# A rotation table for the S5 layer: built in place between the experts of the first expert stage, instead of during the input projection with a trip through DRAM

## What is computed

```python
mag = jnp.exp(dt * a_r)
ab_re = mag * jnp.cos(dt * a_i)
ab_im = mag * jnp.sin(dt * a_i)
...
_, _, hr, hi = lax.associative_scan(combine, (a_re_b, a_im_b, bu_re, bu_im), axis=1)
```

## Time and profile before

| what | us |
|---|---|
| median of 3 runs | 1224.56 (1222.78 to 1225.12) |
| the profiled execution, its own time | 1224.22 |
| its span, first to last instruction | 1222.4 |
| busy in it: PE, DVE, POOL, ACT | 932.2, 449.6, 300.4, 186.0 |
| mean granted TensorE clock | 0.817 of full speed |

### The profile page before, as it was taken

One profiled execution on the slowest core, in us unless ns is written; L12 is line 12 of the kernel. 1 busy time (PEld: TensorE's weight loads), 2 busy tenths in 40 slices (PEclk: granted clock), 3 DMA queues, 4 the chain that ended last, 5 costly groups with the idle time before them and its releaser, 6 DMA issues.

```text
span 1222.4 us, 11170 instructions
## 1 busy us (share of the span) xinstructions
PE 932.2 (76%) x4366; PEld 546.2 (45%) x4366; DVE 449.6 (37%) x757; ACT 186.0 (15%) x313; POOL 300.4 (25%) x439
## 2 busy tenths in 40 slices
PE   7999947988886488888778528999743987787870
PEld 5888737775642233333323427964211333233330
DVE  4899974535124411111011247620254111111116
ACT  1311300121111111111001323210111110011111
POOL 3799915502002321111110210000031111111110
PEclk9999966897578689898889755559955998888895
DMA  9457273020403779999999742430172899999953
GB/s 234 143 202 252 108 237 138 1 78 10 139 14 142 305 272 388 407 412 414 410 409 418 306 121 70 138 103 10 67 289 92 348 409 407 406 410 406 421 223 140
DMA packets 77797, 290.28 MB, mean 237 GB/s; under 512 B 25913, under 2 KB 44807, under 8 KB 62486
## 3 DMA queue, kind: packets, MB, share of 16 engines
q1 hardware_dynamic: 63530, 260.45, 55.4%
q10 hardware_dynamic: 9092, 20.42, 4.9%
q0 software_dynamic: 5120, 8.66, 2.1%
HBM read 267.92 MB, written 28.50 MB: 242 GB/s over the span
## 4 chain that ended last, share of the span: by engine, by line
PE 63%; DVE 20%; issue 8%; DMA 5%; ACT 2%; SPq 1%; POOLq 0%; POOL 0%; ACTq 0%; DVEq 0%
PE ps L1592 20%; PE ps L1611 9%; PE ps L2145 5%; PE ps L1574 3%; DVE work L478 3%; PE ps L838 2%; PE ps L316 2%; PE ps L2008 2%; PE ps L2023 2%; DMA ring<-s_out_mats 2%; DVE work L1121 1%; DVE ring L1124 1%; PE ps L551 1%; PE ps L817 1%; PE ps L565 1%
## 5 line engine op out<-in xcount | busy, mean ns | idle before, releaser
L1592 PE MATMUL ps<-ring,work 128*64 128x512 f32 x512 | 256.6, 660 | 76.8 <-issue 75.4
L1593 PE MATMUL ps<-ring,work 128*64 128x512 f32 x512 | 257.1, 660 | 0.0
L1592 PEld LDWEIGHTS ps<-ring,work 128*64 128x64 f32 x512 | 74.8, 152 | 223.1 <-issue 220.8
L1632 DVE TENSOR_TENSOR work<-ps,work 64x512 f32<-64x512 f32 x32 | 34.1, 1066 | 348.0 <-ACT work L1621 348.0
L1611 PE MATMUL ps<-ring,work 128*64 128x512 f32 x256 | 116.6, 598 | 1.4 <-DVE work L1637 1.4
L1612 PE MATMUL ps<-ring,work 128*64 128x512 f32 x256 | 116.6, 598 | 0.0
L316 PE MATMUL ps<-work,ring 128*128 128x264 f32 x512 | 115.2, 387 | 0.0
L316 PEld LDWEIGHTS ps<-work,ring 128*128 128x128 f32 x512 | 96.8, 190 | 16.4
L1128 POOL TENSOR_TENSOR ring<-ring 128x512 f32<-128x512 f32 (+6 forms) x88 | 96.8, 1118 | 5.7 <-DVE ring L1107 2.1
L1654 POOL COPY work<-work 64x1 int32<-64x1 int32 x32 | 5.7, 178 | 289.6 <-PE ps L1574 243.5
L1593 PEld LDWEIGHTS ps<-ring,work 128*64 128x64 f32 x512 | 74.7, 152 | 0.0
(11 more groups left out here) (456 smaller groups left out, 1367.8 us busy)
## 6 DMA issues: line engine op xcount, KB each, us to landing
ring<-in_moe_w_gate SPq DMA_DIRECT2D x32, 2048.0 KB
ring<-in_moe_w_up SPq DMA_DIRECT2D x32, 2048.0 KB
ring<-in_moe_w_down SPq DMA_DIRECT2D x32, 2048.0 KB, 24.3
ring<-in_w_in ACTq DMA_DIRECT2D x6, 2048.0 KB, 9.0
s_out_mats<-ring SPq DMA_DIRECT2D x4, 1280.0 KB, 4.9
ring<-s_out_mats SPq DMA_DIRECT2D x1, 5120.0 KB, 22.9
ring<-in_w_in SPq DMA_DIRECT2D x2, 2048.0 KB, 10.3
s_in_mats<-ring SPq DMA_DIRECT2D x4, 1024.0 KB, 6.0
```

What stands on the lines that cost most here:

```text
L1592: nc.tensor.matmul(ps[0:SLOT, 2 + s, :], xgT[s][:, c], gate_w[s][:, c], start=c == 0, stop=c == DC - 1)
L1593: last = nc.tensor.matmul(ps[SLOT:P, 2 + s, :], xgT[s][:, c], up_w[s][:, c], start=c == 0, stop=c == DC - 1)
L1632: nc.vector.tensor_tensor(hid[s][0:SLOT].rearrange("t (c p) -> t p c", c=4), strided(ps[SLOT:P, 2 + s, :]), strided(sg[s][SLOT:P]), ALU.mu ...
```

## The change

The table is no longer made during the projection, stored and loaded. `s5_turn_dve`, its store, the wait for the store and `s5_turn_load` are gone. POOL's two squarings move from `s5_prep_pool` to the end of `s5_early_pool`, with three products in place of four (ten instructions on 32 to 64 elements per partition, in four dependent groups). DVE fills `E5` in place during the first expert stage: the start after expert 1's copy of the hidden rows, then one part of one doubling (three instructions) after that of each of the experts 2 to 13. POOL's first copies out of the B matrices after that stage (`s5_mat_pool`) wait for the table, since its scratch lies there. In `ring`, the scratch tiles of the preparation lie elsewhere.

```diff
@@ ab_dve_project
                                   ps[0:11, 5:8, :]).then_inc(*dv.done("conv_rest"))
-            s5_turn_dve(v)
@@ s5_prep_pool
-            nc.gpsimd.tensor_copy(turn[:, 0], pcols[:, 0:2]).then_inc(*po.done())
...
-            cmul(one(1), one(0), one(0), 1)
-            cmul(one(2), one(1), one(1), 1, "turn4")
             cmul(W8[:, :, 2:4], W8[:, :, 0:2], W8[:, :, 1:2], 2)
@@ s5_prep_stores
-            q.wait_ge(*dv.at("turns"))
-            q.dma_start(E_dram, E_ab.rearrange("p w t n -> p (w t n)")).then_inc(sem("E_out"), 16)
             q.wait_ge(sem("cols_out"), 16)
-            q.wait_ge(sem("E_out"), 16)
@@ moe_dve
                 dve_hidT(v, l, *at_expert(k))
+                if l == 0 and k == 1:
+                    s5_turn_start(v)
+                if l == 0 and 2 <= k < 14:
+                    s5_turn_step(v, (k - 2) // 2, k % 2)
@@ s5_turn_load and the functions in its place
-        def s5_turn_load(q):
-            q.wait_ge(sem("stores_S"), 16)
-            q.dma_start(E5.rearrange("p w t n -> p (w t n)"), E_dram).then_inc(sem("E_in"), 16)
+        def s5_turn_start(v):
+
+            v.wait_ge(*po.at("turn4"))
+            v.wait_ge(sem("stores_S"), 16)
+            nc.vector.tensor_copy(E5[:, :, :, 0].rearrange("p w (r k) -> p w r k", r=4),
+                                  turn[:, 1].rearrange("p w (k r) -> p w r k", r=4)).then_inc(*dv.done())
+
+        def s5_turn_step(v, b, w):
+
+            n = 2 ** b
+            tmp = [view(work, F["Bb"] + 1024 * i, PT, 32) for i in range(2)]
+            re, im = (E5[:, i, :, 0:n] for i in range(2))
+            cr, ci = (E5[:, i, :, n - 1:n].to_broadcast([P, PT, n]) for i in range(2))
+            (x, y), (z, o), op = (((re, cr), (im, ci), ALU.subtract), ((re, ci), (im, cr), ALU.add))[w]
+            v.wait_ge(*dv.last())
+            nc.vector.tensor_tensor(tmp[0][:, :, 0:n], x, y, ALU.mult).then_inc(*dv.done())
+            nc.vector.tensor_tensor(tmp[1][:, :, 0:n], z, o, ALU.mult).then_inc(*dv.done())
+            v.wait_ge(*dv.last())
+            nc.vector.tensor_tensor(E5[:, w, :, n:2 * n], tmp[0][:, :, 0:n], tmp[1][:, :, 0:n], op).then_inc(*dv.done("turns"))
@@ s5_early_pool
             tt(abh[:, 1], T8[:, 2], T8[:, 3], ALU.add, "abh")
+            pool.wait_ge(*po.last())
+            x, t = pcol[:, 0:2], T8[:, 0]
+            for i in range(2):
+                for j, (a, b) in enumerate(((0, 0), (1, 1), (0, 1))):
+                    tt(t[:, j], x[:, a], x[:, b], ALU.mult)
+                pool.wait_ge(*po.last())
+                tt(turn[:, i, 0], t[:, 0], t[:, 1], ALU.subtract)
+                tt(turn[:, i, 1], t[:, 2], t[:, 2], ALU.add, "turn4")
+                pool.wait_ge(*po.last())
+                x = turn[:, i]
@@ s5_mat_pool
             pool.wait_ge(sem("Bm_in"), 16)
+            pool.wait_ge(*dv.at("turns"))
@@ s5_dve
-            v.wait_ge(sem("E_in"), 16)
             v.wait_ge(*po.at("abh"))
@@ the SP list
             sp.wait_ge(*pe.at("mixAB2"))
-            s5_turn_load(sp)
             moe_weights(sp, "n0", 0)
```

More of the change, by code:

```diff
@@ L959, in ab_stores @@
                 sp.dma_start(out["s_C"][:, 0, h].rearrange("b k v -> k b v"), Cst[:, h * NS:(h + 1) * NS]).then_inc(sem("stores_C"), 16)
-        S5P = carve(ring, 0, rows=2560, cols=256, ldt=8, W8=512, ZW=256, P5=480, turn=192, Bn=1024, CT=1024,
-                    E=4096, stB=2048, stC=2560)
+        S5P = carve(ring, 0, rows=2560, cols=256, ldt=8, W8=512, ZW=256, P5=480, Bn=1024, CT=1024,
+                    Cn=2048, stB=2048, stC=2560)
         assert S5P["end"] <= 16384, S5P["end"]
@@ L975, in build @@
         P5 = view(ring, S5P["P5"], 3, 5, PT)
-        turn = view(ring, S5P["turn"], 3, 2, PT)
         Bn = view(ring, S5P["Bn"], 2, PT, C5)
-        Cn = view(ring, S5P["E"], 2, DC, 2, N5)
+        Cn = view(ring, S5P["Cn"], 2, DC, 2, N5)
         CT = view(ring, S5P["CT"], 2, PT, C5)
-        E_ab = view(ring, S5P["E"], 2, PT, N5)
         stB = view(ring, S5P["stB"], 2, DC, 4, 2, C5)
         stC = view(ring, S5P["stC"], 2, DC, 5, 2, C5)
-        E_dram = dram("turns", (P, 2 * PT * N5))
         B_dram = dram("s5_in_mats", (4, P, 2048))
@@ L1107, in s5_ct_dve @@
                     nc.vector.tensor_copy(CT[at, :, 8 * n:8 * n + 8], src).then_inc(*dv.done(f"CT{n}"))
[L1109 to L1124, removed]
         def s5_prep_pool(pool):
@@ L1148, in s5_prep_pool @@
             pool.wait_ge(*po.last())
-            one = lambda i: turn[:, i].unsqueeze(2)
-            cmul(one(1), one(0), one(0), 1)
-            cmul(one(2), one(1), one(1), 1, "turn4")
             cmul(W8[:, :, 2:4], W8[:, :, 0:2], W8[:, :, 1:2], 2)
@@ L1808, in build @@
         K1 = carve(work, A["raw"], abh=2 * PT * NS, pcol=8 * PT, h0s=2 * NS * PT, dI=DC * 32, hs=2 * PT * NS, hl=2 * PT,
-                   hout=6 * P, mag=2 * PT, id4=3 * 32)
+                   hout=6 * P, mag=2 * PT, id4=3 * 32, turn=4 * PT)
         assert K1["end"] <= A["cv"], K1["end"]
@@ L1819, in build @@
         id4 = view(work, K1["id4"], 3, 32)
+        turn = view(work, K1["turn"], 2, 2, PT)
         F = carve(work, M["end"], Bb=2048, E=4096, m4=2048)
```

## The result

Before and after, in four runs each: 1224.84 us (1222.78 to 1225.94) and **1206.99 us** (1206.20 to 1207.59). The ratio is 0.9856, interval 0.9839 to 0.9873: the change takes 17.9 us off, more than the 14.5 of the forecast and inside its range. The profiled execution after took 1207.26 us, with a span of 1205.5.

The account below looks back on a forecast made before the run. State loads waiting for DVE's table and its store were taken to bound the stretch before line 551. 14.9 us earlier there, less 0.4 for the routing, made 14.5: 1209.7 profiled, median 1210.0, range 1203.5 to 1216.5.

Parts of the forecast that it names:

- The landing in place of the table's wait: Between the last batch's store and the first state load: the store lands in 4.9 us (4.4 to 5.5).
- POOL's batches: POOL's work before the last store: 3.5 us earlier, 3.0 from batches beside a silent DVE, 0.5 from fewer products.
- The far end: Upper bound for the gain in POOL's batches: 6 us, at 2 ns per element, as line 730 with DVE idle.
- Load to line 551: From the first state load's issue to PE's start of line 551: kept at 18.0 us.
- The floor: PE ends lines 523 to 543 at 165.9, 4.6 us before the states; the gain cannot pass 19.5 us.
- The routing: POOL's ten moved instructions delay its two memsets, which can hold DVE's routing: cost 0.4 us (0 to 2.3).
- The expert stage and the load that was removed: DVE's steps hide in a 7.04 us idle gap, cost 0; removing the 2 MB load gains 0, at most 5.4.
- A: POOL had paid for the whole table: line 551 starts 19.5 us earlier, 19.1 in all, 1205.4; chance 0.16.
- B: POOL gains nothing and the memsets cost the full 2.3 us: 7.8 us faster, 1216.7; chance 0.13.
- C: Table steps in DVE's list between experts fall on the experts' path: 3.5 us slower, 1228.1; chance 0.03.
- D: Another store or load takes the table's place in SP's list, and nothing changes; chance 0.02.
- The rule: DVE and POOL share ports under an exclusive lock; taken strictly, POOL would have lost the whole of every table instruction.

## Why the prediction was right

**What bounded the stretch.** Right. Store of the last batch, wait for the table, its store, eight loads, line 551: that chain is what the change cut, and line 550 is still released by a state load. Either half left as it was costs about the same: a store kept with the table gone takes 6.0 us of the 16.5 back, a table kept with its store off the path 5.9.

**The places.** Forecast from the start of line 514: the last store at 6.7 us, the first load at 11.6, line 551 at 29.6. Measured 7.1, 11.6 and 28.4.

**The landing in place of the table's wait.** Forecast 11.4 from a landing of 4.9; measured 11.8, because this store landed in 4.44, the near end of the bound. That is the difference of 0.4.

**POOL's batches.** Forecast 3.5 us earlier, 3.0 of it in the batches; measured 3.1 in three runs of three. Of that, C3 is 1.9 to 2.0, just the difference of the earlier trace rows. Of the 0.5 for the small products and the 1.1 for the rest of the stretch from 113 to 151, 1.2 came: against the common point B2's store went out 0.7 earlier, C2's 0.8, B3's 1.2 and C3's 3.1. Before any batch the gain is already 0.7; the 0.5 was for that. The choice of C2 as the nearest row was good, and the rows say why: from the store before it to its own C2 took 11.80 us before and 11.75 after, so the table's steps of up to 64 elements beside it had cost POOL next to nothing. The far end, which goes by a row of another line, would have missed.

**Load to line 551.** This term was mis-sized. I kept 18.0 us because DMA had nothing else under way then. It took 16.7 to 16.8 in three runs of the changed kernel. The store experiments show that about 1.1 to 1.5 of the 18.0 us go with a further store just ahead of the loads, whatever its size. So the step "I keep that" was 1.3 us off; what in the transfers makes it is open.

**The floor.** Right in kind, wrong in size. Forecast: line 551 at 165.9, 25.0 us behind the common point, and so 19.5 us of gain at most. With the S loads first line 551 started at 165.66, but in an execution that had begun 1.6 us later: that it looks like 165.9 is chance. From the common point it is 23.2 us and 23.1, a gain of 21.3, past the limit. The forecast took PE's times from the kernel before, and the clock sets them: line 519 took 6.99 us there, where the grant fell to 0.50 soon after 147, and 5.46 with the S loads first, where it fell soon after 150. In the changed kernel line 542 ended 23.0, 24.7 and 24.7 us behind the common point. The forecast itself did not rest on this, since the states decided.

**The routing.** Forecast a cost of 0.4 us; there was none. POOL's memsets ran from 395.40 to 397.24 and DVE's instruction of line 1394 started in the midst of it, with its usual 0.21 us. From there to POOL's first index copy it took 16.33 us (396.57 to 412.90), and 16.36 before (410.55 to 426.91):

```profile
395.40 1.84 POOL L1662 MEMSET work<- 128x1024 f32 x2
```

```profile
396.57 0.21 DVE L1394 TENSOR_TENSOR work<-work 128x48 f32<-128x48 f32 x1
```

The copy of the earlier trace rows, from which the charge was taken, is no model for it: that was a copy, this is a product of two tiles in SBUF.

**The expert stage and the load that was removed.** Forecast 0 and 0, and the remainder of the execution is within its spread. Four times the steps cost no more than 1 to 2 us. The load behind the removed one was issued at 393.68 instead of 411.46, 3.8 us beyond the common shift of 14.0 there, without effect.

**The sum.** 14.9 forecast against 16.2 measured at line 551: +0.4 landing, +1.3 loads, -0.4 POOL. With the measured terms, and nothing for the routing, the sum is 1224.2 - 16.2 = 1208.0; the two repeats gave 1208.6 and 1208.3. The profiled execution behind the first comparison's 1207.0 has a remainder 2.3 us shorter than before, which the repeats don't show.

**The rivals.** A, that POOL had paid for the whole table, asked for a store near 139 and no wait at 551: the store went out at 149.48, and PE waited 5.33. B asked for 151.1, 10.2 us behind the common point, and a cost in the routing: the store went out at 7.1, and the routing cost nothing. C is refuted by the run that made it happen. D is not the case.

**The rule.** POOL's instruction of 7.03 us, which had started first, held DVE's of 0.19 for 6.80 us, and POOL itself took 7.04 without that company. That is how the Trainium skill, page "SBUF — State Buffer", section "SBUF: two separate sides", has it, an exclusive lock that the first comer keeps for its whole instruction. The same section names which DVE instructions take part: those with two operands in SBUF count only against a GpSimd operation that reads SBUF. The traces agree: line 1394 was not held by a memset (0.21 us), and the products of lines 705 and 707, one operand of which is in PSUM, kept 0.67 to 0.69 us beside line 747 where that ran from 183.37 on. What the strict reading gets wrong here is the size: POOL lost 0.33 and 0.15 us in each of its instructions of C3 (1863 against 1530 ns, 1486 against 1338), 1.9 us in all, beside eight table instructions (three of 256 elements, five of 512) that take some 4.7 us together with POOL idle, at the 0.42 and 0.69 us of the expert stage after. DVE lost more: beside C3 a table instruction of 512 elements took 1.7 to 2.0 us, more than one of 1024 with POOL idle (1.22). One such row of the kernel before:

```profile
143.82 2.02 DVE L1122 TENSOR_TENSOR work<-ring 128x512 f32<-128x512 f32 x1
```

Why the loss falls so unevenly is not settled by these runs.

## What to carry to other kernels

When a store or a wait is taken off a queue, look for what waits at the same place for the same producer through another engine: here SP waited for the table by a semaphore and PE by DVE's order, and leaving either would have cost 6 of the 16.5 us. A step can be put for nothing into the idle gap of an engine in a stage bound by transfers if its largest piece is under the gap; even at four times the size it cost 1 to 2 us here. And a consumer that waits for a whole set of loads may need only half of it: splitting the semaphore gave another 5.8 us, the best step behind this change (1202.45 us; with POOL's scaling later 1200.47, which is not told apart from it).

## What was not expected of the hardware

- Eight loads of 512 KB kept PE waiting until 16.7 to 16.8 us behind their first issue, and until 17.9 to 18.3 us when one store more, of 2 MB or of 256 KB, had landed right before. The DMA engines moved 290 GB/s in both cases, but 0.4 to 0.6 MB more by then with the further store. Open.
- The beginning of the execution differs by up to 1.5 us from run to run: PE's line 297 began at 19.96 us before and at 21.44 after, with the same instructions of PE up to there, because the matmuls of line 293 went over from 647 to 386 ns each some 3 us later. The views give a granted clock of 1.00 for this stretch in both, so they don't show the change; the durations do. Two kernels are better compared from a point behind it.
- 64 narrow matmuls (two columns each, a full weight load each) took 13.81 us at a granted clock of 0.50, and 12.03 us at a mean of 0.58 where they began 2 us ahead of its fall. Idle time of PE ahead of them made no difference: 13.81 us behind 5.3 us of it, 13.81 behind 3.7, 13.78 behind none.
- A POOL instruction that reads SBUF holds a DVE product of two SBUF operands for all its time, 6.80 us instead of 0.19, while a POOL memset does not. But taking the hold away brought less than could be measured, since POOL then became the late one.
